# Modulation products of a two-layer diffusion step, spread over four 32-column strips of the PE array

## What is computed

```python
def modulation(cvec, l):
    m = jax.nn.silu(cvec) @ w_mod[l] + b_mod[l]
    return m.reshape(cvec.shape[0], N_MOD, D_MODEL)

def half_ffn(x, j, s):
    h = modulate(rmsnorm(x, g[2 * s]), mod[:, 3 * s], mod[:, 3 * s + 1])
    y = swiglu(h, p['ffn_w1'][l, j], p['ffn_w3'][l, j], p['ffn_w2'][l, j])
    return x + 0.5 * mod[:, 3 * s + 2][:, None] * rmsnorm(y, g[2 * s + 1])
```

## Time and profile before

| | |
|---|---|
| median of 3 runs | 3538.85 us (3532.32 to 3545.0) |
| profiled execution, its span | 3552.6 us |
| time recorded for it beside the span | none |
| TensorE busy | 3246.1 us (91%) |
| VectorE busy | 1176.9 us (33%) |
| GpSimd busy | 1142.8 us (32%) |
| ScalarE busy | 526.0 us (15%) |
| granted TensorE clock, mean | 0.932 |

### The profile page before, as it was taken

How to read it: one execution, slowest core, us unless ns; L and a number is a source line. 1 busy time by engine, 2 the same in 40 slices (tenths; PEclk the granted TensorE clock), 3 DMA queues, 4 the chain that set the end, 5 groups by cost and what they waited for, 6 DMA issues and landing times.

```text
span 3552.6 us, 49289 instructions
## 1 busy us (share of the span) xinstructions
PE 3246.1 (91%) x20936; PEld 2961.8 (83%) x20936; DVE 1176.9 (33%) x1612; ACT 526.0 (15%) x866; POOL 1142.8 (32%) x388
## 2 busy tenths in 40 slices
PE   7999999788888979999789999997798889799997
PEld 3889889778777879999748898897787778799996
DVE  3110111443465454133231101114534554531332
ACT  2000001301212230001120000012011122300011
POOL 1334334222112224454313343342221122244442
PEclk9999999888788989999899999998797789899998
DMA  6322332110101012221152223221110010122211
GB/s 240 118 114 81 119 118 85 61 50 28 42 31 60 25 48 71 77 75 64 38 209 107 107 104 114 109 87 53 48 38 30 30 60 33 44 71 73 83 59 59
DMA packets 45631, 271.92 MB, mean 77 GB/s; under 512 B 5121, under 2 KB 10753, under 8 KB 19521
## 3 DMA queue, kind: packets, MB, share of 16 engines
q1 hardware_dynamic: 38736, 259.99, 20.5%
q10 hardware_dynamic: 6768, 10.11, 0.8%
HBM read 265.35 MB, written 4.73 MB: 76 GB/s over the span
## 4 chain that ended last, share of the span: by engine, by line
PE 42%; DVE 4%; ACT 1%; issue 1%; DMA 1%; DVEq 1%; ACTq 0%; PEldq 0%; SPq 0%
PE ps L456 12%; PE ps L458 11%; PE ps L457 11%; PE ps L466 3%; PE ps L649 1%; DMA first_raw<-in_w_mod 1%; ACT arena L849 1%; PE ps L617 1%; PE ps L656 1%; DVE arena L1188 1%; PE ps L608 1%; PE ps L634 0%; DVE xT L1191 0%; DVE rstd L1155 0%; PE ps L819 0%
## 5 line engine op out<-in xcount | busy, mean ns | idle before, releaser
L456 PE MATMUL ps<-h,wsplit 128*128 128x320 f32 (+1 forms) x3520 | 1104.8, 314 | 29.5 <-DVE h L1171 20.0
L457 PE MATMUL ps<-h,wsplit 128*128 128x320 f32 (+1 forms) x3520 | 1093.1, 311 | 0.0
L458 PE MATMUL ps<-h,wsplit 128*128 128x320 f32 (+1 forms) x3520 | 1093.0, 311 | 0.0
L415 POOL TENSOR_SCALAR wsplit<-raw 128x2048 fp32r<-128x2048 f32 (+1 forms) x192 | 332.7, 1733 | 2351.2 <-issue 1046.7
L417 POOL TENSOR_TENSOR wsplit<-raw,wsplit 128x2048 fp32r<-128x2048 f32 (+1 forms) x192 | 809.9, 4218 | 16.0
L456 PEld LDWEIGHTS ps<-h,wsplit 128*128 128x128 f32 (+1 forms) x3520 | 663.2, 188 | 53.7 <-issue 41.3
L457 PEld LDWEIGHTS ps<-h,wsplit 128*128 128x128 f32 (+1 forms) x3520 | 663.7, 189 | 0.5
L458 PEld LDWEIGHTS ps<-h,wsplit 128*128 128x128 f32 (+1 forms) x3520 | 663.2, 188 | 0.5
L456 PE MATMUL ps<-hidden,wsplit 128*128 128x320 f32 x1408 | 436.3, 310 | 4.8 <-DVE hidden L1203 4.8
L458 PE MATMUL ps<-hidden,wsplit 128*128 128x320 f32 x1408 | 435.1, 309 | 0.0
L457 PE MATMUL ps<-hidden,wsplit 128*128 128x320 f32 x1408 | 435.0, 309 | 0.0
(11 more groups left out here) (172 smaller groups left out, 2919.2 us busy)
## 6 DMA issues: line engine op xcount, KB each, us to landing
raw<-in_w SPq DMA_DIRECT2D x88, 1024.0 KB, 5.0
raw<-in_w_mod SPq DMA_DIRECT2D x48, 1024.0 KB, 4.8
raw<-in_w SPq DMA_DIRECT2D x64, 704.0 KB, 4.1
raw<-in_w_in SPq DMA_DIRECT2D x30, 1024.0 KB, 4.8
first_raw<-in_w_mod SPq DMA_DIRECT2D x24, 1024.0 KB, 4.8
raw<-in_w_out SPq DMA_DIRECT2D x8, 1024.0 KB, 4.9
arena<-in_rpb ACTq DMA_DIRECT2D x2, 1792.0 KB, 8.5
xT<-in_x ACTq DMA_DIRECT2D x1, 2560.0 KB, 11.7
```

The costliest lines, as they stand in the source:

```text
L415: nc.gpsimd.tensor_scalar(w[:, 0], src, 1.0, 1.0, ALU.mult, ALU.mult).then_inc(pool_hi, 1)
L456: mm(out, w[0], x[0], start=first, stop=False)
L457: mm(out, w[0], x[1], start=False, stop=False)
L458: return mm(out, w[1], x[0], start=False, stop=last)
```

## The change

The 8 products of a unit go to four places in turn. Product k writes its two rows at partition 32 * (k % 4), so that four partial sums of two products each arise at partitions 0, 32, 64 and 96. The copy to `mrow` takes all 128 partitions. The two transposes are replaced by two products: stationary is 128 x 128 of `mrow`, moving a constant `pick` of 128 x 2, which is 1 where the partition modulo 32 is 0 (first column) or 1 (second column), and 0 elsewhere; it adds up the four partial rows and turns them in one. Since the copy now also reads partitions that no product has written, PSUM is set to 0 once at the beginning, on VectorE, in the first block, at whose end the engines meet. The number and size of the loads of weights stay as they are.

```diff
--- before.py
+++ after.py
@@ -74,7 +74,7 @@
 _at = 0
 for _name, _w in (("ident", P), ("ones", P), ("rope", NT * 2 * HD), ("namask", HD), ("causal", 2 * P),
                   ("anti", 2 * P), ("block", P), ("blockn", SW), ("diff", 2 * P), ("posrow", 2 * P),
-                  ("poscol", 2), ("carry", NTOK)):
+                  ("poscol", 2), ("carry", NTOK), ("pick", 2)):
     CONSTS[_name] = (_at, _w)
     _at += _w
 CONST_W = _at
@@ -340,6 +340,10 @@
                 act.activation(cond, cond, ACT.Silu).then_inc(cond_ready, 1)
                 act.wait_ge(cond_ready, 1)
 
+            @block.vector
+            def _(dve):
+                nc.vector.memset(ps[:, :], 0.0)
+
         with nc.Fori(0, DEPTH) as l:
             with nc.Block() as block:
 
@@ -463,8 +467,9 @@
                         pe.wait_ge(unit_evac, i * du + (n + 1))
                         w = tiles(slot_ap(n, SLOT_W), KT)
                         for k in range(KT):
-                            last = mm(ps[0:2, half(n):half(n) + 256], cond[:, k, :], w[:, k, :],
-                                      start=k == 0, stop=k == KT - 1)
+                            strip = slice(k % 4 * 32, k % 4 * 32 + 2)
+                            last = mm(ps[strip, half(n):half(n) + 256], cond[:, k, :], w[:, k, :],
+                                      start=k < 4, stop=k >= 4)
                         last.then_inc(unit_done, 1)
 
                     def mod_turn(n, q, i=0):
@@ -473,7 +478,7 @@
                         pe.sem_inc(turn_begun, 1)
                         for m in range(2):
                             c = half(n) + BANK + 2 * m
-                            last = pe.transpose(ps[:, c:c + 2], mrow[0:2, m * P:(m + 1) * P], ident[0:2, 0:2])
+                            last = mm(ps[:, c:c + 2], mrow[:, m * P:(m + 1) * P], C("pick"), start=True, stop=True)
                         last.then_inc(mtr_done, 1)
 
                     def sums(v, n=None):
@@ -1121,7 +1126,7 @@
                     def mod_rows(n, i2):
 
                         dve.wait_ge(unit_done, i2 * 2 + UD(n))
-                        V.tensor_copy(mrow[0:2, :], ps[0:2, half(n):half(n) + 256]).then_inc(mrow_ready, 1)
+                        V.tensor_copy(mrow, ps[:, half(n):half(n) + 256]).then_inc(mrow_ready, 1)
 
                     def mod_cols(n, q, i1=0):
 
@@ -1714,6 +1719,7 @@
     put("diff", np.stack([np.maximum(i[None] - j, 0), np.maximum(j - i[None], 0)], 1))
     put("posrow", np.broadcast_to(np.stack([i + 1, P - i]), (P, 2, P)))
     put("poscol", np.stack([P - 1 - i, i], 1))
+    put("pick", i[:, None] % 32 == np.arange(2)[None])
     put("carry", np.broadcast_to(np.arange(NTOK) % P != 0, (P, NTOK)))
     return c
 
```

## The result

The changed kernel takes 3445.22 us (median of 4 runs, 3442.24 to 3452.21), the kernel before 3541.93 in the runs beside it. The ratio is **0.9715**, 95% interval 0.9694 to 0.9737. The interval of the 3438 is some 3431 to 3446, so it reaches into the range; the size of the gain is what was missed.

What follows compares the result with a forecast made beforehand. TensorE was taken as the bound, with every modulation unit in the loops on the path. 85.3 - 30.7 + 22 - 1 = 75.6 us off the median 3538.85 gave 3463 us, range 3442 to 3500.

Steps and rivals of the forecast that it cites:

- The strips overlap, four at a time: Modulation products, line 466: four run at once, 0.86 us and a tail of 0.17, 1.03 per unit; chance 0.57.
- Strict order: Modulation products: records start in program order, gain 1.52 us instead of 1.83, 3482 us; two at a time included, chance 0.20.
- The PSUM half as the new bound: In the loops the next up-projection waits until VectorE frees its PSUM half; 1.83 us gained at each of 44 places.
- The turn: Two fp32 products replacing two transposes: 0.94 us instead of 0.30, 0.64 more, 48 turns in the loops, 30.7 us lost.
- My lower bound for the term: Turn in the loops: 0 more per turn, if all weight loads overlap; the upper bound was 0.9 more.
- The range: Whole kernel: low end 97 us off, 3442; high end about 38 us off, 3500.
- Before the loops: Stretch ahead of the feed-forward loops: shorter units gain 11 us per layer at a rather low clock, 22; ends 0 and 32.
- The memset: Zeroing PSUM on VectorE in the first block: 4.3 us, mostly hidden behind loads; cost 0 to 2, taken as 1.
- A mode change that drains: Entry into a modulation unit: changing tiling mode drains the engine; at a doubled price 9 us, inside the range.
- The queues: SP's load order and GpSimd's split in the loops: some 3 us of slack stay, so neither becomes the bound.
- gaps between up- and down-projections: In the loops: 80.5 us from 44 gaps after up-projections and 4.8 from those after down-projections, sum 85.3.

Runs made afterwards that it cites:

- Early SiLU: The changed kernel with ScalarE's SiLU waiting for the gate products only and VectorE's product for the whole unit; 3417.68 us, ratio 0.9652.
- turn twice: The changed kernel with each of the turn's two products made twice, four records more per turn; 3480.12 us, ratio 0.9829.
- turn with two rows: New turn and memset without strips, the turn's products taking only rows 0 and 1 instead of 128 rows; 3568.23 us in one run.
- fillers: The changed kernel with three unread fp32 products of 256 columns behind each turn of a layer's first 11 units; 3446.85 us, ratio 0.9725.
- two strips: The changed kernel with the 8 products of a unit going to two strips instead of four; 3467.11 us, ratio 0.9772.

## Why the prediction was right and wrong

- **The strips overlap, four at a time**: right, as taken. 1.04 us for a unit, where 1.03 was worked out. Strict order, the rival with 3482 us, is out for column strips: the trace has the first records of four products ahead of the second record of the first one. The Trainium skill, TensorE: Matmul & The Clock Gate, "Packing small matmuls", has matmuls start and end in program order; the prediction read that for the single records, and then a unit would take 8 x 0.215 + 0.38 = 2.1 us. Measured is 1.04, so it doesn't hold for the records of fp32 products, which are two each. Read for whole products, nothing in the trace speaks against it.
- **The PSUM half as the new bound**: right. 1.96 us between up-projections means 1.82 gained, 1.83 was the term. Early SiLU takes the wait away, and the time falls as it should.
- **The turn: this is the step that failed.** "Line 649 has the nearest price, 1.78 us of weight load for 8, 0.222 each" gave 0.64 us more per turn and a loss of 30.7 us. Measured: 0.04 more, 1.8 us for 48 turns. Two things were wrong. The price was read in a stretch at the lower clock. The windows view of the kernel before has it, and beside it stands that of the changed kernel's loops:

```profile
2728.00:2748.00 20.00, 18.22 (x86) 17.03 (x87) 9.12 (x14) 1.48 (x3) 0.00 (x0) 0.50 0.00 1
```

```profile
1800.00:2240.00 440.00, 425.60 (x3093) 405.40 (x3093) 54.10 (x98) 32.07 (x45) 181.52 (x62) 1.00 0.33 120
```

  Line 649's row starts at 2733.29, in the middle of that. In the loops the clock is 1.00, and a record of the turn takes 0.112 (turn twice), half of 0.222. And "0.09 for the wait" was counted for the new turn as for the old, but it belongs to the two rows and went with them (turn with two rows). 4 x 0.112 with the first load hidden is 0.36, against the 0.30 of the transposes. The 28.9 us of this term are more than the whole miss of 25. My lower bound for the term, no extra at all, would have been the better value.
- **The range**: its low end was added up wrongly. "full clock before the loops (32) and a turn only 0.24 longer instead of 0.64 (19)" is 85.3 - 11.5 + 32 - 1 = 104.8 us and so 3434, not 97 and 3442. By its own terms the range would have held the 3438. That doesn't mend the step above: inside it the turn would still have been taken at 0.24 instead of 0.04, with a full clock before the loops that didn't come.
- **Before the loops**: 22 us forecast, 15.5 in the profiles. The mechanism was right: the clock stays low there (0.57 in the window above; a unit of 1.89 us where 1.9 was taken). Its ends, 0 and 32, held it. The size was not: at half clock 11.7 per layer were worked out, and 8.6 and 7.0 came. In the second layer, from the first unit to the third 1.1 us were gained where 3 were taken, over the three cycles up to unit 8 4.3 instead of 5.2, from there to the scales 1.2 instead of 1.7, and from the scales to the first FFN product 0.9 instead of 1.8; the first unit also started 0.6 later. What the profile after shows in addition: the turn at the low clock is 1.01 us, the norm sum of 4 records 2.48 instead of 1.34, and units wait for loads and for the turn's addition, which stands behind VectorE's squares. Whether the full clock would have given the 16 us is open (fillers). In the first layer the clock has to be read from the durations: between 18 and 48 us the column says 1.00 for the changed kernel, but its units take 1.89 us there, and its trace has no record of the clock before 50.7 us.
- **The memset**: cost nothing that shows. SP goes on at 5.69 instead of 3.87, as worked out, but the first unit starts at 16.82, before it was 17.25: the loads in front of it were still under way. I had taken 1 us.
- **A mode change that drains**: the entry into a unit is 0.24 us after the last record, as before. The four strips cost nothing more at the entry. 0.24 is the entry into records with 2 columns of weights (a unit) or 2 rows (the transposes, the turn with two rows); into the turn with 128 x 128, the shape of the up-projection's own weights, it is 0.15. The Trainium skill, TensorEngine Tiling (Array Packing), "Key Properties", says that a change of tiling mode drains the engine. The trace agrees in direction, at 0.09 for an entry; no run here tells a drain from another reason.
- **The queues**: right. Neither SP's order nor GpSimd's split became a wait in the loops, even with early SiLU at 15.70 (between 1800 and 2240 us TensorE waits for the split once, 0.2 us).

Sum of terms, forecast and measured: gaps between up- and down-projections 85.3, turns -30.7, before the loops 22, memset -1, against 81.5 for the loops with turns (of which the turns are -1.8, so the gaps are 83) and 15.5 with the memset: 97 us. The ratio gives 101, with 93 to 108. So the turn was 28.9 too dear, and the gaps and what is before the loops together 9 too good; that these two lay the other way is luck, and it kept the miss at 21 to 25.

## What to carry to other kernels

A price taken from a row holds for the clock of that row: look at the granted clock of the stretch before a duration is used elsewhere, or a weight load is counted at twice its price. When a piece of work between two users of the same buffer is shortened, ask first what it covered; here two strips were enough in the loops, and the next gain was a semaphore that let ScalarE start on the half of the data that was ready. Small products that fill few columns ran in four strips at once in fp32 too, and the helper product cost least in the shape of its neighbours.

## What was not expected of the hardware

- An fp32 product with 2 rows of weights costs 0.28 us more per turn of two than the same with 128 rows, and 0.24 instead of 0.15 us to its first record (two runs that differ in nothing else).
- The token mixing, the same instructions in all of these kernels, took from 608 to 622 us in the 20 layers profiled, and both layers of one execution differ from each other too (621.8 and 613.6; 613.8 and 621.3). What goes with it is TensorE's granted clock, which changes often between its two levels there. One of the shortest of the 20, in the profile of early SiLU, and the longest, in that of two strips, have it at 0.86 and 0.83 of the full clock on average, with the same number of matmul records:

```profile
587.10:1195.50 608.40, 518.42 (x3441) 478.98 (x3441) 306.62 (x487) 128.69 (x233) 134.35 (x40) 0.86 0.12 41
```

```profile
611.10:1233.00 621.90, 533.62 (x3441) 492.82 (x3441) 307.02 (x487) 128.61 (x233) 135.42 (x40) 0.83 0.12 41
```

Over all 20 the time at the lower level goes from 171 to 209 us, and the length follows it closely (correlation 0.98, about 0.4 us for each). The four of the changed kernel, profiled twice, lie between 610.6 and 621.8. So a difference of 10 us between two profiled spans of this kernel can be that alone, and the span difference of 110.6 us contains 13.7 of it; without them it is 97, as the terms add up to. Why the clock falls differently in each execution stays open.
